# First attention: squares of the head outputs and their products with root and gate on Pool for three of four token tiles

## The chip, the cores and the metric

The kernel runs on one core of a Trainium2 chip. The core has five engines that run side by side and meet at semaphores: TensorE (PE in the profile), VectorE (DVE), ScalarE (ACT), GpSimd (POOL) and SyncE (SP, which issues loads here). The metric is the device time of one execution in microseconds (us), lower is better.

## The reference, cut to what matters

The program is a whole model of three blocks: a differential attention, a latent attention (MLA), and a block with dilated attention, convolution and 32 experts, on 512 tokens of width 1024. The change touches only the end of the first attention:

```
def _diff_attention(h, positions, ...):
    ...
    def block(qb):
        sc = einsum('bqhcd,bkhcd->bhcqk', qb, k) * scale
        p = softmax(sc, axis=-1)
        p = p[:, :, 0] - lam * p[:, :, 1]
        return einsum('bhqk,bkhd->bqhd', p.astype(v.dtype), v)
    o = _from_blocks(lax.map(block, _to_blocks(q)))
    o = _rmsnorm(o, subln_g) * (1.0 - lambda_init)
    o = o.reshape(b, s, DA_WIDTH) * silu(z)
    return o @ w_out
```

For each token and each of 8 heads, the 128 outputs are squared, summed, turned into one over the root of the mean, and multiplied with that root and with the gate silu(z). All is float32.

## The kernel before, in words

The work is staged for one core with weights streamed through a ring of slots. The first attention runs in 32 steps, one for each pair of token tile t (4 tiles of 128 tokens) and head h (8). Each engine has its own program; what follows is the order in which each issues one step i.

PE (`attention`, lines 650 to 680): the scores of step i + 2 (line 795, two banks of 512 columns), four transposes of the combined probabilities of step i (line 601), and the product with V of step i - 1 (line 799). When i is 6 in a tile (OUT_AT), it also transposes the gated outputs of the tile before (`out_tile`, line 722 waits for `og_ready`, then eight transposes at line 601), between the transposes and the product.

DVE (`attention`, lines 1738 to 1749): the row maxima of step i + 1 (`maxima0`, line 1821, 1024 columns from PSUM), then `combine0` of step i: a reciprocal (line 1828), a small product (line 1829, two inputs and a scalar in SBUF), and the difference of the two softmaxes (line 1832, 512 columns, two inputs in SBUF) which PE's transposes of step i wait for. Then `post0` of step i - 2 (line 1838): the head output from PSUM into `o_raw`.

ACT: the exponentials of step i + 1 (line 1155) and copies of the transposes (line 1164; line 1179 for gated outputs).

In `post0`, when h is 7, DVE also squares the 1024 columns of the tile (line 1846, into `bufE`) and sums them by head (line 1847, into `ss`). POOL waits for the sums and makes the root in six small instructions on 8 columns (`rstd`, lines 1409 to 1419). When h is 1 in the next tile, DVE calls `finish_heads`: eight products of 128 columns, o_raw times root times gate into `D_tok` (line 1856), then `og_ready` (line 1859). For the last tile `finish_heads` follows at once.

POOL otherwise does little here: its program around the change is the two stores of zeros (line 1440), then the loop over four tiles with `norm_rstd` (line 1443), then the roots of the later norms. SP's queue waits for `og_ready` only at line 523, for the 12th of its increments in the whole kernel.

In the rows, buffers have the names of the tensors that hold them: `slots` holds `o_raw`, `bufE`, the probabilities and V; `bufD` holds `D_tok` under its own view; `mix` holds the combined probabilities, `pw` and `ss` the small columns of the roots.

Of the kernel before, what the change touches and what calls it, by code (L numbers as in the profile page):

```python
# [10 lines left out]
ALU = mybir.AluOpType  # L11
ACT = mybir.ActivationFunctionType
AX = mybir.AxisListType

P = 128
T = 512
TT = T // P
D = 1024
# [3 lines left out]
HEADS = 8  # L22
# [20 lines left out]
MAIN = sum(ROWS_OF)  # L43
LN_AT = 4
OUT_AT = 6
PAIRS_OUT_AT = 3
GATED = ((0, slice(0, T // 2)), (1, slice(0, T // 2)), (0, slice(T // 2, T)), (1, slice(T // 2, T)), (2, slice(0, T)), (3, slice(0, T)))
OVER = 16
# [90 lines left out]
def fused_kernel(nc, a, out, xs, ys):  # L139

    with ExitStack() as ctx:
# [3 lines left out]
        def sem(name):  # L145
            return ctx.enter_context(nc.semaphore(name))
# [9 lines left out]
        bufE = slots[:, late:late + 2560]  # L156
# [21 lines left out]
        ss = sb("ss", [P, 16])  # L178
# [29 lines left out]
        C_tok, D_tok = tok(bufC), tok(bufD)  # L208
        o_raw = hT.rearrange("p b n -> p (b n)").rearrange("p (t n) -> p t n", t=TT)
# [88 lines left out]
        squares_ready, rstd_ready = sem("squares_ready"), sem("rstd_ready")  # L298
# [6 lines left out]
        max_ready, exp_ready, mix_ready = sem("max_ready"), sem("exp_ready"), sem("mix_ready")  # L305
        og_ready, oT_ready, convT_ready = sem("gated_output_ready"), sem("outputT_token_tile_ready"), sem("convT_ready")
        raw1_ready, n1_ready, nT_ready = sem("latents_ready"), sem("latents_normed"), sem("latentsT_ready")
        qk_ready = sem("qk_ready")
        norm_row_in, norm_row_used = sem("norm_row_loaded"), sem("norm_row_used")
        alibi_in = sem("alibi_loaded")  # L310
        sig_ready, u_used = sem("sigmoid_ready"), sem("sigmoid_used")
# [1087 lines left out]
        def _(pool):  # L1399
            steps = Steps(pool, pool_step)  # L1400
            gp = nc.gpsimd
# [21 lines left out]
            def norm_rstd(width=D, cols=TT, arrivals=TT, lo=0):  # L1423
                nonlocal count
                count += arrivals
                pool.wait_ge(squares_ready, count)
                rstd(cols, width, lo)

            def tile_rstds(*cols):
                for col in cols:  # L1430
                    norm_rstd(D, 1, 1, col)
# [6 lines left out]
            for rows in (xs[:, :], ys[MAIN:, :]):  # L1438
                blocks = rows.rearrange("(p m) d -> p m d", p=ZERO_P)
                gp.dma_start(blocks, norm_row[0:ZERO_P, :].unsqueeze(1).to_broadcast([ZERO_P, blocks.shape[1], D]))\  # L1440
                    .then_inc(zeros_out, 16)
            for t in range(TT):
                norm_rstd(128, 8, 1)
            tile_rstds(0, 1, 2, 3)
            norm_rstd(1, 8, 1)
            tile_rstds(0, 1, 4, 5, 2, 6, 3, 7)
# [40 lines left out]
        def _(dve):  # L1487
# [11 lines left out]
            def wait_rstd():  # L1499
                rstds[0] += 1  # L1500
                dve.wait_ge(rstd_ready, rstds[0])
# [333 lines left out]
            def post0(i):  # L1835
                t, h = i // HEADS, i % HEADS
                bank = dve_banks.take(dve)
                v.tensor_scalar(o_raw[:, t, h * P:(h + 1) * P], bank[:, 0:P], inv_sums[:, 2 * i:2 * i + 1], None,
                                ALU.mult).then_inc(dve_freed, 1)
                if h == 1 and t > 0:  # L1840
                    finish_heads(t - 1)
                if h == HEADS - 1:

                    dve.wait_ge(dve_freed, dve_banks.n)
                    sq = bufE[:, 0:D]
                    chain(v.tensor_tensor(sq, o_raw[:, t, :], o_raw[:, t, :], ALU.mult))
                    v.tensor_reduce(ss[:, 0:8], sq.rearrange("p (h d) -> p h d", h=HEADS), AX.X, ALU.add)\
                        .then_inc(squares_ready, 1)
                    if t == TT - 1:
                        finish_heads(t)  # L1850

            def finish_heads(t):
                wait_rstd()
                for h in range(HEADS):
                    zt = D_tok[:, t, h * P:(h + 1) * P]
                    steps(v.scalar_tensor_tensor(out=zt, in0=o_raw[:, t, h * P:(h + 1) * P], scalar=ss[:, h:h + 1],
                                                 in1=zt, op0=ALU.mult, op1=ALU.mult))
                steps.settle()
                dve.sem_inc(og_ready, 1)
# [338 lines left out]
```

## Time and profile before

| | |
|---|---|
| median of 3 runs | 1653.33 us (1652.55 to 1653.66) |
| the profiled execution's own time | 1656.97 us |
| its span, first to last instruction | 1655.2 us |
| busy in the span | PE 1424.4 us, DVE 644.3, ACT 357.5, POOL 103.5 |
| first attention, first maxima to last head output | 277.0 to 384.8 us |
| mean granted TensorE clock | 0.936 of full speed |

The profile is one execution; its time is 3.6 us over the median, and what it is read for is the length and order of things inside it. Times in rows are us from the start of the span. In a timeline row the columns are start, duration, engine, line, operation, what it writes and reads, and in brackets the engine's idle time just before with the instruction that ended it. In a row of stretches, each engine has its busy time and number of instructions, then PEclk (the granted TensorE clock, 1.00 is full speed, 2.4 GHz), the busy share of the DMA engines and GB/s.

### The profile page before, as it was taken

The numbers are of one execution on the slowest core, as the hardware profiler recorded it, in microseconds if no ns is written. First come the engines' busy times: TensorE is split into PE (matmuls) and PEld (weight loads), VectorE is DVE, ScalarE is ACT, GpSimd is POOL, SyncE is SP. The second block draws the span as 40 slices with busy tenths as digits, with TensorE's granted clock in tenths as the row PEclk, the third lists the DMA queues.
The fourth block names the chain that finished last, engine by engine and source line by source line (L and its number), as shares of the span: only waits on it lengthen the run. The fifth ranks groups of instructions, "written<-read, shape, count | busy, mean of one in ns | idle before, by whom it ended". The sixth has DMA issues, their size and how long they took to land.

```text
span 1655.2 us, 17036 instructions
## 1 busy us (share of the span) xinstructions
PE 1424.4 (86%) x6498; PEld 724.4 (44%) x6498; DVE 644.3 (39%) x1170; ACT 357.5 (22%) x778; POOL 103.5 (6%) x236
## 2 busy tenths in 40 slices
PE   4999999889899999999899989969986876968770
PEld 2544444554455444664654456424432333423330
DVE  4664102994357413322489763242211111111113
ACT  2434002762311143431400163100000000000001
POOL 3000000010100000001100000120000000000004
PEclk9999999999999899999899989979998989979985
DMA  9762224920267431002424123269999999999984
GB/s 341 272 212 81 97 102 158 313 61 1 92 230 236 154 135 69 1 1 102 155 74 152 51 102 153 76 230 395 413 400 409 407 406 401 417 401 412 401 360 156
DMA packets 101339, 356.98 MB, mean 216 GB/s; under 512 B 9448, under 2 KB 15641, under 8 KB 92681
## 3 DMA queue, kind: packets, MB, share of 16 engines
q1 hardware_dynamic: 82512, 305.15, 48.5%
q0 software_dynamic: 9728, 34.47, 6.2%
q10 hardware_dynamic: 9016, 16.25, 2.7%
q8 instruction: 54, 0.88, 0.2%
q14 instruction: 29, 0.23, 0.0%
HBM read 323.60 MB, written 32.24 MB: 215 GB/s over the span
## 4 chain that ended last, share of the span: by engine, by line
PE 64%; DMA 17%; DVE 11%; ACT 2%; issue 2%; SPq 1%; POOL 1%; ACTq 0%; DVEq 0%; POOLq 0%
PE bank L625 15%; DMA slots<-in_w_exp_up 12%; PE score_banks L617 11%; PE score_banks L1006 9%; PE score_banks L625 9%; DVE bufD L1976 5%; PE bank L601 4%; PE bank L1016 4%; DMA slots<-in_w_exp_gate 2%; PE bank L859 2%; PE score_banks L795 2%; PE score_banks L852 2%; DMA slots<-in_ada_w 2%; PE bank L799 2%; SPq L508 1%
## 5 line engine op out<-in xcount | busy, mean ns | idle before, releaser
L625 PE MATMUL bank<-slots 128*128 128x512 f32 x608 | 265.8, 595 | 4.4 <-ACTq L1182 2.5
L617 PE MATMUL score_banks<-slots 128*128 128x512 f32 (+1 forms) x584 | 249.3, 586 | 11.4 <-ACTq L1108 6.2
L1006 PE MATMUL score_banks<-slots,norm_row 128*64 128x512 f32 (+1 forms) x768 | 174.4, 631 | 54.8 <-DMA slots<-in_w_exp_up 47.4
L625 PEld LDWEIGHTS bank<-slots 128*128 128x128 f32 x608 | 114.4, 191 | 146.7 <-issue 143.4
L617 PEld LDWEIGHTS score_banks<-slots 128*128 128x128 f32 x584 | 114.2, 198 | 139.6 <-issue 129.8
L625 PE MATMUL score_banks<-slots 128*128 128x512 f32 (+1 forms) x384 | 157.3, 570 | 0.6 <-PE bank L625 0.3
L2076 DVE TENSOR_TENSOR mix<-probsT,score_banks 128x256 f32<-128x256 f32 (+1 forms) x39 | 14.4, 370 | 326.6 <-ACT probsT L1374 326.6
L1006 PEld LDWEIGHTS score_banks<-slots,norm_row 128*64 128x64 f32 (+1 forms) x768 | 60.3, 148 | 162.9 <-issue 162.8
L1016 PE MATMUL bank<-slots,mix 128*64 128x512 f32 (+1 forms) x864 | 115.2, 477 | 11.5 <-issue 10.4
L1374 ACT ACTIVATE probsT<-score_banks 128x256 f32<-128x256 f32 (+1 forms) x39 | 13.4, 343 | 464.2 <-PE score_banks L1006 464.2
L625 PEld LDWEIGHTS score_banks<-slots 128*128 128x128 f32 x384 | 74.5, 200 | 77.7 <-issue 77.7
L1006 PE MATMUL score_banks<-slots,mix 128*32 128x256 f32 (+1 forms) x960 | 77.7, 451 | 31.1 <-issue 29.4
L1976 DVE SCALAR_TENSOR_TENSOR bufD<-slots,col,bufD 128x512 f32<-128x512 f32 x120 | 80.5, 746 | 0.4
L1016 PEld LDWEIGHTS bank<-slots,mix 128*64 128x64 f32 (+1 forms) x864 | 45.0, 121 | 66.1 <-issue 60.8
L1006 PEld LDWEIGHTS score_banks<-slots,mix 128*32 128x32 f32 (+1 forms) x960 | 39.7, 127 | 73.2 <-issue 60.7
L1637 DVE SCALAR_TENSOR_TENSOR bufD<-slots,silu_c,bufD 128x512 f32<-128x512 f32 x91 | 68.4, 752 | 4.1 <-DMA slots<-in_w_mod 0.6
L1711 DVE TENSOR_TENSOR mix<-bank,gate_row 128x512 f32<-128x512 f32 x24 | 16.6, 692 | 119.9 <-PE bank L625 119.7
L1821 DVE TENSOR_REDUCE negmax<-score_banks 128x2 f32<-128x1024 f32 x32 | 39.0, 1221 | 61.3 <-PE score_banks L795 60.6
L1637 DVE SCALAR_TENSOR_TENSOR slots<-slots,silu_c 128x512 f32<-128x512 f32 x70 | 52.6, 752 | 11.3 <-DMA slots<-in_w_mod 5.8
L1409 POOL TENSOR_SCALAR pw<-ss 128x1 f32<-128x1 f32 (+2 forms) x27 | 8.1, 299 | 768.0 <-ACT slots L1096 439.7
L601 PE MATMUL bank<-k_sb,slots 128*128 128x128 f32 x312 | 48.0, 297 | 8.0 <-ACTq L1107 3.8
L601 PEld LDWEIGHTS bank<-k_sb,slots 128*128 128x128 f32 x312 | 36.7, 150 | 32.1 <-issue 19.5
(295 smaller groups left out, 1480.9 us busy)
## 6 DMA issues: line engine op xcount, KB each, us to landing
slots<-in_w_exp_down SPq DMA_DIRECT2D x32, 2048.0 KB, 36.1
slots<-in_w_exp_gate SPq DMA_DIRECT2D x32, 2048.0 KB, 30.4
slots<-in_w_exp_up SPq DMA_DIRECT2D x32, 2048.0 KB, 32.7
slots<-in_w_in SPq DMA_DIRECT2D x16, 2048.0 KB, 8.6
slots<-in_w_mod SPq DMA_DIRECT2D x24, 1024.0 KB, 5.2
slots<-in_ada_w SPq DMA_DIRECT2D x18, 1024.0 KB, 7.2
expert_rows<-norm_row POOLq DMA_DIRECT2D x1, 12672.0 KB, 50.4
slots<-in_w_out SPq DMA_DIRECT2D x6, 2048.0 KB, 7.9
```

Of the source, the lines that this page charges most:

```text
L601: last = nc.tensor.transpose(bank[:, i * P:(i + 1) * P], piece, ident)
L617: last = mm(bank[:, cols], w[:, k, lo:lo + P], src[:, k, cols], start=(k == 0), stop=(k == kts - 1))
L625: last = mm(bank[:, 0:cols], src[:, k, t * P:(t + 1) * P], rhs(k), start=(k == 0), stop=(k == kts - 1))
L795: return mm(bank[:, :], A8[r, h, t * P:(t + 1) * P], B8[r, h, :], start=True, stop=True)
L799: last = mm(bank[:, 0:P], pT[:, j * P:(j + 1) * P], C_tok[:, j, h * P:(h + 1) * P], start=(j == 0), stop=(j == TT - 1))
L852: mm(bank[:, :], hT[:, 2 * pair + c, t * P:(t + 1) * P], A8[:, 2 * pair + c, :], start=True, stop=False)
L859: last = mm(bank[:, c * P:(c + 1) * P], pT[:, j * P:(j + 1) * P], C_tok[:, j, h * P:(h + 1) * P], start=(j == 0), stop=(j == TT - 1))
L1006: last = mm(out, rows[:, k, :], e_gu[it.p][:, :, k, c * pc.ff:(c + 1) * pc.ff], start=(k == 0), stop=(k == KT - 1))
L1016: last = mm(psum[6 + pc.bank][c * pc.size:(c + 1) * pc.size, 0:pc.cols], hTe[pc.bank][:, lo:lo + pc.size], e_down[it.p][:, f, c * pc.cols: ...
L1637: return v.scalar_tensor_tensor(out=acc, in0=w, scalar=c, in1=acc, op0=ALU.mult, op1=ALU.add)
L1821: v.tensor_reduce(negmax[:, 2 * i:2 * i + 2], pair, AX.X, ALU.max, negate=True).then_inc(max_ready, 1)
L1976: conv_at[j] = steps(v.scalar_tensor_tensor(out=conv[:, j, :], in0=src, scalar=wcol, in1=conv[:, j, :], op0=ALU.mult, op1=ALU.add))
```

## The change

For tiles 0 to 2, the squares and the products with root and gate go from DVE to POOL. DVE signals `heads_ready` after the tile's last head output. POOL then squares the tile in one instruction of 1024 columns into `bufE`. DVE sums the squares two steps later, behind the post of head 1 of the next tile (`SQUARES_AT`), after waits on the squares and, from tile 2 on, on an earlier `og_ready`. POOL makes the root as before, then multiplies `o_raw` with the root (1024 columns, in place, root broadcast along 128 columns), waits for that, and multiplies `D_tok` with it (1024 columns), which raises `og_ready`. Tile 3 stays on DVE.

```
--- before.py
+++ after.py
@@ -43,6 +43,7 @@
 MAIN = sum(ROWS_OF)
 LN_AT = 4
 OUT_AT = 6
+SQUARES_AT = 1
 PAIRS_OUT_AT = 3
 GATED = ((0, slice(0, T // 2)), (1, slice(0, T // 2)), (0, slice(T // 2, T)), (1, slice(T // 2, T)), (2, slice(0, T)), (3, slice(0, T)))
 OVER = 16
@@ -305,7 +306,8 @@
         max_ready, exp_ready, mix_ready = sem("max_ready"), sem("exp_ready"), sem("mix_ready")
         og_ready, oT_ready, convT_ready = sem("gated_output_ready"), sem("outputT_token_tile_ready"), sem("convT_ready")
         raw1_ready, n1_ready, nT_ready = sem("latents_ready"), sem("latents_normed"), sem("latentsT_ready")
-        qk_ready = sem("qk_ready")
+        qk_ready, heads_ready = sem("qk_ready"), sem("heads_of_tile_ready")
+        head_squares = sem("squares_of_heads_ready")
         norm_row_in, norm_row_used = sem("norm_row_loaded"), sem("norm_row_used")
         alibi_in = sem("alibi_loaded")
         sig_ready, u_used = sem("sigmoid_ready"), sem("sigmoid_used")
@@ -1440,7 +1442,16 @@
                 gp.dma_start(blocks, norm_row[0:ZERO_P, :].unsqueeze(1).to_broadcast([ZERO_P, blocks.shape[1], D]))\
                     .then_inc(zeros_out, 16)
             for t in range(TT):
+                if t < TT - 1:
+                    pool.wait_ge(heads_ready, t + 1)
+                    gp.tensor_tensor(bufE[:, 0:D], o_raw[:, t, :], o_raw[:, t, :], ALU.mult).then_inc(head_squares, 1)
                 norm_rstd(128, 8, 1)
+                if t < TT - 1:
+                    heads = o_raw[:, t, :].rearrange("p (h d) -> p h d", h=HEADS)
+                    pool.wait_ge(rstd_ready, 2 + t)
+                    steps(gp.tensor_tensor(heads, heads, ss[:, 0:8].unsqueeze(2).to_broadcast([P, HEADS, P]), ALU.mult))
+                    steps.settle()
+                    gp.tensor_tensor(D_tok[:, t, :], D_tok[:, t, :], o_raw[:, t, :], ALU.mult).then_inc(og_ready, 1)
             tile_rstds(0, 1, 2, 3)
             norm_rstd(1, 8, 1)
             tile_rstds(0, 1, 4, 5, 2, 6, 3, 7)
@@ -1837,19 +1848,28 @@
                 bank = dve_banks.take(dve)
                 v.tensor_scalar(o_raw[:, t, h * P:(h + 1) * P], bank[:, 0:P], inv_sums[:, 2 * i:2 * i + 1], None,
                                 ALU.mult).then_inc(dve_freed, 1)
-                if h == 1 and t > 0:
-                    finish_heads(t - 1)
+                if h == SQUARES_AT and t > 0:
+                    if t > 1:
+                        dve.wait_ge(og_ready, t - 1)
+                    dve.wait_ge(head_squares, t)
+                    sum_squares()
                 if h == HEADS - 1:
-
                     dve.wait_ge(dve_freed, dve_banks.n)
+                    if t < TT - 1:
+                        dve.sem_inc(heads_ready, 1)
+                        return
                     sq = bufE[:, 0:D]
                     chain(v.tensor_tensor(sq, o_raw[:, t, :], o_raw[:, t, :], ALU.mult))
-                    v.tensor_reduce(ss[:, 0:8], sq.rearrange("p (h d) -> p h d", h=HEADS), AX.X, ALU.add)\
-                        .then_inc(squares_ready, 1)
-                    if t == TT - 1:
-                        finish_heads(t)
+                    dve.wait_ge(og_ready, t)
+                    sum_squares()
+                    finish_heads(t)
+
+            def sum_squares():
+                v.tensor_reduce(ss[:, 0:8], bufE[:, 0:D].rearrange("p (h d) -> p h d", h=HEADS), AX.X, ALU.add)\
+                    .then_inc(squares_ready, 1)
 
             def finish_heads(t):
+                rstds[0] += t
                 wait_rstd()
                 for h in range(HEADS):
                     zt = D_tok[:, t, h * P:(h + 1) * P]
```

## Rows read from the trace of the kernel before

**Rows 1.** The page's first line: the span of the profiled execution.

```profile
span 1655.2 us, 17036 instructions
```

**Rows 2.** Stretches between the squares of one tile and the next: length, busy us per engine, PEclk.

```profile
307.70:334.31 26.61, 21.68 (x138) 14.15 (x137) 24.46 (x51) 17.63 (x43) 2.67 (x6) 1.00 0.90 287
334.31:361.41 27.10, 23.19 (x138) 15.52 (x137) 24.55 (x50) 17.52 (x43) 2.65 (x6) 0.94 0.25 77
361.41:384.40 22.99, 18.14 (x117) 13.81 (x116) 18.84 (x40) 12.65 (x30) 2.65 (x6) 0.93 0.00 1
```

**Rows 3.** Timeline, undisturbed attention step on PE and DVE (start us, us, engine, line, op).

```profile
302.47 1.22 DVE L1821 TENSOR_REDUCE negmax<-score_banks 128x2 f32<-128x1024 f32 x1
...
303.79 1.13 PE L795 MATMUL score_banks<-slots 64*128 64x512 f32 x4
303.81 0.22 DVE L1829 SCALAR_TENSOR_TENSOR inv_sums<-inv_sums,lam,sums 128x1 f32<-128x1 f32 x1
304.06 0.75 DVE L1832 SCALAR_TENSOR_TENSOR mix<-slots,inv_sums 128x512 f32<-128x512 f32 x1
...
304.73 0.35 DVE L1838 TENSOR_SCALAR slots<-bank,inv_sums 128x128 f32<-128x128 f32 x1
...
305.06 1.23 DVE L1821 TENSOR_REDUCE negmax<-score_banks 128x2 f32<-128x1024 f32 x1
...
306.35 1.13 PE L795 MATMUL score_banks<-slots 64*128 64x512 f32 x4
```

**Rows 4.** PE's waits between 277 and 388 us: total, times, longest.

```profile
PE bank L601 <- DVE mix L1832: 12.9, 7, 2.4
```

**Rows 5.** Timeline around tile 0's squares and products.

```profile
307.70 1.23 DVE L1846 TENSOR_TENSOR slots<-slots 128x1024 f32<-128x1024 f32 x1
...
308.96 1.22 DVE L1847 TENSOR_REDUCE ss<-slots 128x8 f32<-128x1024 f32 x1
310.10 1.21 DVE L1821 TENSOR_REDUCE negmax<-score_banks 128x2 f32<-128x1024 f32 x1
...
312.48 0.66 PE L601 MATMUL bank<-k_sb,mix 128*128 128x128 f32 x4 [2.41 <-DVE mix L1832]
...
312.60 1.22 DVE L1821 TENSOR_REDUCE negmax<-score_banks 128x2 f32<-128x1024 f32 x1
...
315.11 2.18 DVE L1856 SCALAR_TENSOR_TENSOR bufD<-slots,ss,bufD 128x128 f32<-128x128 f32 x8
...
317.50 1.22 DVE L1821 TENSOR_REDUCE negmax<-score_banks 128x2 f32<-128x1024 f32 x1 [0.21 <-DVE bufD L1856]
```

**Rows 6.** One-microsecond stretch after tile 1's squares (PEclk is the third last number).

```profile
339.00:340.00 1.00, 0.92 (x5) 0.92 (x6) 1.00 (x3) 0.40 (x2) 0.69 (x4) 0.50 0.49 152
```

**Rows 7.** Timeline of POOL, three of six instructions for tile 0's root.

```profile
310.28 0.20 POOL L1409 TENSOR_SCALAR pw<-ss 128x8 f32<-128x8 f32 x1 [31.14 <-DVE ss L1847]
310.56 1.67 POOL L1411 TENSOR_TENSOR pw<-pw,half_neg 128x8 f32<-128x8 f32 x1
...
313.17 0.20 POOL L1419 TENSOR_TENSOR ss<-pw 128x8 f32<-128x8 f32 x1
```

**Rows 8.** POOL's product by shape, between 420 and 1100 us (busy us, mean ns).

```profile
L1415 POOL TENSOR_TENSOR pw<-pw 128x1 f32<-128x1 f32 x16 | 3.1, 191 | 1.3
```

**Rows 9.** The same line by shape, between 277 and 394 us.

```profile
L1415 POOL TENSOR_TENSOR pw<-pw 128x8 f32<-128x8 f32 x4 | 0.8, 203 | 0.3
```

**Rows 10.** Timeline of POOL near 782 us: two small instructions that ran long.

```profile
781.90 1.28 POOL L1409 TENSOR_SCALAR pw<-ss 128x1 f32<-128x1 f32 x1
...
784.71 0.74 POOL L1419 TENSOR_TENSOR ss<-pw 128x1 f32<-128x1 f32 x1
```

**Rows 11.** Timeline of DVE over the same moments.

```profile
781.85 1.28 DVE L1626 SCALAR_TENSOR_TENSOR x<-x,ss,norm_row 128x1024 f32<-128x1024 f32 x1 [1.81 <-POOL ss L1419]
...
784.71 0.69 DVE L1714 TENSOR_TENSOR x<-x,mix 128x512 f32<-128x512 f32 x1
```

**Rows 12.** Timeline, DVE's first reduction after the output transposes of tile 0.

```profile
329.13 1.23 DVE L1821 TENSOR_REDUCE negmax<-score_banks 128x2 f32<-128x1024 f32 x1 [0.81 <-PE score_banks L795]
```

## The prediction

> **What bounds the kernel now.** I read the page first: the span is 1655.2 us [rows 1], and the profiled execution took 1656.97 us against a median of 1653.33. I make the sums as differences from the profiled execution and carry them over to the median; the 3.64 us between the two are not explained by anything here and drop out. Then I cut the attention into its three periods from one tile's squares to the next one's. They last 26.61, 27.10 and 22.99 us, the last one without most of the scores of a next tile [rows 2]. DVE is busy in more than nine tenths of the first two, PE in some 22 of 27 us.
>
> Next the timeline of one quiet step. PE begins the scores every 2.56 us. DVE begins its maxima every 2.59 us, and goes from maxima to the small product in 1.34 us, to the difference in another 0.25, to the head output in 0.67, to the next maxima in 0.33 [rows 3]. Behind a disturbance DVE repeats in 2.50 us (310.10 to 312.60) [rows 5]. So the two engines are tied: DVE can catch up 0.06 us a step and no more, and whatever is put into DVE's step, PE waits for. The waits say so: PE stood 12.9 us in 7 waits for the difference, the longest 2.4 [rows 4].
>
> The timeline shows where. The squares and their sum hold DVE from 307.70 to 310.10, and PE's next transposes sit idle 2.41 us. The eight products hold it from 315.11 to 317.50 [rows 5]. That is 2.40 + 2.39 = 4.79 us of DVE a tile, three times (tile 3's come when no step is behind them). There is a second price. After tile 1's squares the granted clock is 0.50 [rows 6], which is 1.2 GHz instead of 2.4, after PE had stood for 2.4 us. The mean clock of the periods says that tile 2 has the same and tile 0 not (1.00, 0.94, 0.93), and the second period is 27.10 - 26.61 = 0.49 us longer than the first [rows 2]. I take 0.49 us for each of two tiles.
>
> **What the change removes and adds on DVE.** Removed a tile: the squares, 1.26 us from their start to that of the sum, and the products, 2.39. The sum stays and moves two steps back, at its 1.14 us from start to start [rows 5]. Net 1.26 + 2.39 = 3.65 us a tile, 10.95 in all. With the sum alone PE stands about 1.1 us rather than 2.4, so the clock may hold too: 0.98 more. If POOL cost nothing, the kernel would be 11.9 us faster. Tile 3 changes nothing but two waits on things long done. The semaphore increment for POOL takes the place of a wait that is there already; I put it at nothing, and at the 0.04 us between two instructions if it isn't. No DMA is added or moved. SP's wait is for the 12th `og_ready`, which still comes from the second attention. On POOL's queue the three products stand ahead of the next roots, whose squares come from ACT some 40 us later: nothing.
>
> **What POOL's instructions cost.** No row has POOL multiply 1024 columns. Its product takes 191 ns on one column [rows 8] and 203 ns on eight [rows 9], so 12 ns for 7 columns, 1.7 ns a column, and 1.95 us for 1024 as an estimate. From below, I see no reason for POOL to beat DVE's 1.22 us for the same shape [rows 5]. From above, 4 ns more in so small a difference would make it 2.5, and I go to 2.6. I take 1.95, since it comes from the same operation on the same engine. The Trainium skill (GPSIMD Engine Reference, section Elementwise, side-by-side cycle accounting) gives 4497 ns for a two-input product of 2048 columns; an estimate by it is 2.25 us, and by that the forecast below would be 2.7 us later. No run here shows it.
>
> Is that time hidden? By waits alone, yes. The squares have from 307.8 until DVE's sum about 5 us later. The roots take from 310.28 to 313.37, 3.1 us [rows 7], and begin 0.1 us after the sum. The sum would begin at 312.8 and end at 314.0; the root is there at 317.2, and two products by 321.3. PE wants them after the transposes of step 6. DVE's difference for that step is two steps and 1.34 + 0.25 + 0.75 us behind the sum's 1.14: 312.8 + 1.14 + 5.0 + 2.34 = 321.3, and the transposes take 0.66 more. So `og_ready` comes 0.6 us early, and at 2.3 us a product just in time. Behind those output transposes DVE stands idle for 0.81 us [rows 12], which would cover a delay; POOL's products are over by then, so it covers none of theirs.
>
> **The port.** What isn't hidden is in the trace far from here. At 781.90 a POOL instruction on one column took 1.28 us instead of 0.19, and at 784.71 another took 0.74 [rows 10]. In those moments DVE ran instructions with two SBUF inputs, 781.85 to 783.13 and 784.71 to 785.40 [rows 11]: POOL's ended when DVE's did, within 0.05 us. So these two exclude each other for the whole of the first one. The rows show only POOL waiting, because POOL's own instructions there are too short to hold DVE. The new ones are long. I take it that the exclusion holds the other way: DVE's small product and difference wait until a POOL product that has begun is over. Maxima, sum and head output have one tensor input, and I let them run on: POOL's instruction at 310.28 lay inside DVE's maxima and took its usual 0.20 us [rows 5, 7].
>
> The Trainium skill says the same and more (SBUF — State Buffer, section Who interferes with whom): the pair of ports is locked for the whole instruction, whoever starts first, and a DVE instruction with two SBUF inputs meets only POOL instructions that read SBUF. The first half agrees with the rows above; the other direction no row here shows.
>
> Worked out for one tile:
> - Squares: POOL starts at 307.8, ends 309.75. DVE's small product is due 1.34 us behind the maxima at 307.7, at 309.04. Delay 0.71.
> - Product with the root: it starts 0.1 + 3.1 + 0.1 = 3.3 us behind the sum's end, that is 4.5 behind its start. DVE has by then done the 1.14 of the sum and 2.50 of one step, so it is 0.86 into a step, 0.48 before the small product. Delay 1.95 - 0.48 = 1.47.
> - Product with the gate: it is issued 0.09 us behind the other, while the small product (0.22 us) runs, and gets the port as that ends, just ahead of the difference, which is due 0.25 us after the small product began. Delay 1.9.
>
> Together 4.1 us against the 3.65 taken away: +0.45 us a tile, +1.35 in three. PE stands 3.4 us in one piece in each tile, longer than the 2.4 after which the clock fell in two of three tiles, so I take the fall in all three: +0.5. Each handing over of the port may cost up to 0.05 us, and is left out. Sum **+1.9 us**, 1655.2.
>
> **The rivals.**
> 1. *No lock against DVE.* DVE's instructions run on beside POOL's long reads. For it: no row shows DVE late behind POOL, and beside the root's power instruction of 1.67 us [rows 7] DVE kept its 2.50 us step (though on 8 columns the reads may be over at once). Against: [rows 10, 11]. Price: -11.9, less up to 0.5 where POOL waits for DVE and `og_ready` is late: 1641.4 to 1642.
> 2. *The difference takes the port ahead of the second product.* 0.05 us decide it. Then the gate product runs from 1.0 to 2.95 us behind the first one's end and meets the next small product at 2.5, for 0.45 us. Delays 0.71 + 1.47 + 0.45 = 2.6, net -1.0 a tile, -3.0 in all: 1650.3. With products of 2.3 us it is 1.06 + 1.82 + 0.80 = 3.7 and 1653.5.
> 3. *POOL is slower than its slope says.* Every further 0.1 us counts three times a tile, 0.9 us in all. The line from the same to slower is crossed at 2.1 us a product. At 2.6: delays 1.36 + 2.12 + 2.55 = 6.0, net +2.4 a tile, +7.1, and the clock: 1661. Broadcasting the root or writing in place are the likeliest reasons.
> 4. *POOL late for PE.* Without the lock this begins at 2.3 us a product and costs twice the excess; with it PE is later anyway. It only trims rival 1.
>
> **How the numbers follow.** A measurement of this kernel can tell about 0.2%, 3.3 us, from no change. Forecast (lock, gate product first, 1.7 to 2.2 us a product, -0.4 to +4.1): 0.40. Rival 1: 0.20. Rival 2: 0.20, half of it beyond -3.3. Rival 3: 0.20, all slower. Of the forecast 0.10 lies beyond +3.3. So faster 0.20 + 0.10, and 0.02 from smaller delays than worked out: 0.32; slower 0.20 + 0.10 = 0.30; same 0.38. The range holds rival 1 at its lower end and rival 3 up to 2.5 us a product: 1641.3 to 1660. The forecast's own range is 1652.9 to 1657.4.
>
> **What the profile after would show.** On POOL, nine products of 1024 columns, about 1.95 us each; longer ones have waited for DVE. DVE's small product and difference starting more than 1.4 us behind their maxima in the steps of those nine. PE's transposes idle for about 0.7 and 3.4 us a tile. The three periods at 27.6, 27.6 and 23.4 us instead of those of [rows 2]; by rival 1 at 23.0, 23.0 and 18.9. I am wrong if DVE keeps its 2.5 us steps while a POOL product runs, or if those products aren't between 1.7 and 2.2 us.

## The result, and the profile after

| | before | after |
|---|---|---|
| median | 1653.33 us (11 runs beside those of after: 1650.62 to 1656.5) | 1657.95 us (11 runs: 1655.28 to 1661.52) |
| ratio | | 1.0029, 95% interval 1.0019 to 1.0040 |
| the profiled execution's own time, its span | 1656.97, 1655.2 us | 1657.03, 1655.2 us |
| first maxima to last head output | 107.5 us | 111.6 us |
| of it, behind the last head output of tile 0 | 77.1 us | 81.8 us |
| time at half clock, 300 to 392 us | 6.8 us | 17.1 us |

The changed kernel's median is 4.6 us higher, 0.29%. That is little: the kernel before, run against itself (e9 below), came out 0.22% apart. The two spans happen to be equal, so the span says nothing; the attention does. From the start of the first maxima to that of the last head output it is 4.1 us longer, 275.9 to 387.5; counted from the last head output of tile 0, behind which the change does its first work, it is 4.7 us longer. The last line of the table adds up what is missing to 1.00 in the granted clock of the one-microsecond stretches from 300 to 392 us, doubled, since each missing piece fell to 0.50.

The page's first lines, the span and the busy time of each engine (share, instructions):

```profile
span 1655.2 us, 17021 instructions
...
PE 1424.4 (86%) x6498; PEld 724.0 (44%) x6498; DVE 644.9 (39%) x1143; ACT 357.5 (22%) x778; POOL 122.8 (7%) x245
```

POOL gained 19 us, and DVE, which lost 10.2 us of squares and products, is as busy as before (644.9 against 644.3). The DVE instructions grouped by line and shape, 277 to 396 us, show where it went (count, then busy us and mean ns of one):

```profile
L1843 DVE SCALAR_TENSOR_TENSOR mix<-slots,inv_sums 128x512 f32<-128x512 f32 x32 | 30.5, 954 | 1.1
L1840 DVE SCALAR_TENSOR_TENSOR inv_sums<-inv_sums,lam,sums 128x1 f32<-128x1 f32 x32 | 11.5, 358 | 1.1
```

The difference took 752 ns each before and the small product 220. Times 32 that is 6.5 and 4.4 us in which DVE's instructions stood begun and blocked. The same view of POOL, 277 to 400 us:

```profile
L1454 POOL TENSOR_TENSOR bufD<-bufD,slots 128x1024 f32<-128x1024 f32 x3 | 7.0, 2339 | 0.2
...
L1452 POOL TENSOR_TENSOR slots<-slots,ss 128x1024 f32<-128x1024 f32 x3 | 5.7, 1896 | 0.2
L1447 POOL TENSOR_TENSOR slots<-slots 128x1024 f32<-128x1024 f32 x3 | 5.7, 1892 | 57.3 <-DVEq L1859 57.3
```

Tile 0 in the timeline, with the steps of three of those nine products:

```profile
306.22 1.89 POOL L1447 TENSOR_TENSOR slots<-slots 128x1024 f32<-128x1024 f32 x1 [28.13 <-DVEq L1859]
...
306.29 1.23 DVE L1832 TENSOR_REDUCE negmax<-score_banks 128x2 f32<-128x1024 f32 x1 [0.21 <-DVE slots L1849]
...
307.62 0.50 DVE L1840 SCALAR_TENSOR_TENSOR inv_sums<-inv_sums,lam,sums 128x1 f32<-128x1 f32 x1
...
308.97 0.66 PE L603 MATMUL bank<-k_sb,mix 128*128 128x128 f32 x4 [0.49 <-DVE mix L1843]
...
315.11 0.66 PE L603 MATMUL bank<-k_sb,mix 128*128 128x128 f32 x4 [0.99 <-DVE mix L1843]
...
316.08 1.90 POOL L1452 TENSOR_TENSOR slots<-slots,ss 128x1024 f32<-128x1024 f32 x1
...
316.55 1.44 DVE L1840 SCALAR_TENSOR_TENSOR inv_sums<-inv_sums,lam,sums 128x1 f32<-128x1 f32 x1
...
318.03 2.91 DVE L1843 SCALAR_TENSOR_TENSOR mix<-slots,inv_sums 128x512 f32<-128x512 f32 x1
318.05 2.34 POOL L1454 TENSOR_TENSOR bufD<-bufD,slots 128x1024 f32<-128x1024 f32 x1
320.86 0.34 DVE L1849 TENSOR_SCALAR slots<-bank,inv_sums 128x128 f32<-128x128 f32 x1
...
320.99 1.12 PE L603 MATMUL bank<-k_sb,mix 128*128 128x128 f32 x4 [3.28 <-DVE mix L1843]
...
321.90 1.92 PE L801 MATMUL bank<-slots,probsT 128*128 128x128 f32 x8
...
323.75 2.08 PE L797 MATMUL score_banks<-slots 64*128 64x512 f32 x4
...
325.97 1.22 DVE L1832 TENSOR_REDUCE negmax<-score_banks 128x2 f32<-128x1024 f32 x1 [1.76 <-PE score_banks L797]
```

Read it in pairs. The squares end at 308.11, and so does the small product, which took 0.50 instead of 0.22: 0.28 late. The product with the root runs from 316.08 to 317.98, and the small product at 316.55 ends with it: 1.22 late. The product with the gate starts at 318.05, between the small product's end and the difference; DVE's next instruction starts at 320.86, 2.83 behind the difference's start, where 0.67 is usual [rows 3]: 2.16 late. A DVE instruction that waits for the port is shown as long, not as idle, which is why the busy time of 644.9 us hides it. None of the three blocked instructions is late by all of the wait: the small products end 0.01 us behind POOL's product and not their usual 0.22, the difference 0.55 behind and not 0.75. It is as if about 0.2 us of each had run while it waited. Then PE: 0.49, 0.99 and 3.28 us idle. PE's waits from 277 to 392 us, beside [rows 4], and the periods beside [rows 2]:

```profile
PE bank L603 <- DVE mix L1843: 14.2, 9, 3.3
```

```profile
306.22:335.48 29.26, 24.25 (x138) 15.87 (x137) 24.76 (x41) 17.52 (x42) 8.80 (x10) 0.88 0.89 277
335.48:363.74 28.26, 23.29 (x138) 15.37 (x137) 24.73 (x41) 17.52 (x42) 8.79 (x9) 0.94 0.18 59
363.74:387.48 23.74, 19.01 (x116) 15.06 (x115) 18.91 (x31) 12.69 (x29) 8.79 (x9) 0.86 0.00 1
```

And the clock from the gate product on (PEclk is the third number from the end):

```profile
318.00:319.00 1.00, 0.00 (x0) 0.00 (x0) 0.97 (x1) 0.00 (x0) 0.95 (x1) 1.00 0.98 319
...
320.00:321.00 1.00, 0.01 (x1) 0.01 (x1) 1.00 (x2) 0.00 (x0) 0.39 (x1) 0.50 0.98 348
...
325.00:326.00 1.00, 1.00 (x3) 0.25 (x2) 0.03 (x1) 0.00 (x0) 0.00 (x0) 0.50 0.79 238
...
327.00:328.00 1.00, 0.75 (x7) 0.55 (x6) 0.93 (x4) 0.98 (x2) 0.00 (x0) 1.00 0.75 176
```

PE stood from 317.7 to 320.99, and the clock went to 0.50, 1.2 GHz, for some 6.8 us, in a tile that had none of it before. The four transposes then took 1.12 us instead of 0.66, the product with V 1.92 instead of 1.06, the scores 2.08 instead of 1.13. Now DVE waits for PE: 1.76 us before its maxima at 325.97, and 0.41 before the head output ahead of them. In tile 0 before, DVE has no wait in that step. The first period is 2.65 us longer than before, and only 0.22 of it is DVE's own.

### The profile page after: what moved, and what is told of

The parts are those of the page before. It is cut to its first block, busy times and chain, and to the rows that moved or that the text cites. A ratio compares the mean times of both kernels' runs of the same rounds, so it can differ in the third digit from the quotient of the medians.

```text
span 1655.2 us, 17021 instructions
## 1 busy us (share of the span) xinstructions
PE 1424.4 (86%) x6498; PEld 724.0 (44%) x6498; DVE 644.9 (39%) x1143; ACT 357.5 (22%) x778; POOL 122.8 (7%) x245
## 4 chain that ended last, share of the span: by engine, by line
PE 62%; DMA 17%; DVE 14%; issue 3%; ACT 3%; SPq 1%; POOL 1%; ACTq 0%; DVEq 0%; POOLq 0%
PE bank L627 15%; DMA slots<-in_w_exp_up 12%; PE score_banks L619 10%; PE score_banks L1008 10%; PE score_banks L627 9%; DVE bufD L1996 5%; PE bank L1018 4%; PE bank L603 3%; DMA slots<-in_w_exp_gate 2%; DVE negmax L1832 2%; PE bank L861 2%; PE score_banks L854 2%; DMA slots<-in_ada_w 2%; SPq L510 1%; DVE mix L1843 1%
## 5 line engine op out<-in xcount | busy, mean ns | idle before, releaser
L619 PEld LDWEIGHTS score_banks<-slots 128*128 128x128 f32 x584 | 113.2, 196 | 140.2 <-issue 130.1
```

Source lines behind the costliest of these rows:

```text
L619: last = mm(bank[:, cols], w[:, k, lo:lo + P], src[:, k, cols], start=(k == 0), stop=(k == kts - 1))
```

## The experiments

The ratios are against runs of the kernel before on the same chip and in the same series; its median there was 1653.61 us beside e1 to e4, 1654.22 beside e5 to e8, 1655.92 beside e9 and e10, and 1654.43 beside e11. So medians of different series are compared by their ratios. "DVE balance" is worked out for one tile from each trace, as a mean over tiles 0 to 2: what DVE is spared (squares 1.26, products 2.39, less 1.13 where it keeps one product) against what its small product and difference took longer than 0.22 and 0.75 us, and 0.21 for the signal behind a tile's last head output, which e2 and e4 don't have. A plus means more time on DVE. "Attention" is first maxima to last head output, "behind tile 0" the part of it from the last head output of tile 0, "half clock" as above.

| run | median us | ratio, 95% interval | attention us | behind tile 0, us | DVE balance a tile, us | half clock us |
|---|---|---|---|---|---|---|
| before | 1653.33 | | 107.5 | 77.1 | 0 | 6.8 |
| after | 1657.95 | 1.0029 (1.0019 to 1.0040) | 111.6 | 81.8 | +0.20 | 17.1 |
| e1 squares only | 1658.01 | 1.0027 (1.0015 to 1.0040) | 106.3 | 77.5 | -0.77 | 10.2 |
| e2 products only | 1657.05 | 1.0023 (1.0009 to 1.0037) | 110.9 | 80.8 | +0.96 | 10.3 |
| e3 memsets | 1642.38 | 0.9927 (0.9910 to 0.9945) | 96.0 | 65.7 | -3.44 | 0 |
| e4 idle products | 1663.57 | 1.0050 (1.0032 to 1.0068) | 116.7 | 87.6 | +2.09 | 13.6 |
| e5 placed | 1648.34 | 0.9963 (0.9945 to 0.9981) | 99.1 | 68.7 | -2.31 | 0 |
| e6 unplaced | 1659.43 | 1.0025 (1.0011 to 1.0039) | 108.9 | 78.5 | +0.02 | 10.3 |
| e7 a step earlier | 1653.84 | 0.9996 (0.9980 to 1.0012) | 107.5 | 77.1 | -0.77 | 10.2 |
| e8 is e1 again | 1656.92 | 1.0011 (0.9995 to 1.0027) | 106.3 | 77.5 | -0.77 | 10.2 |
| e9 is before again | 1651.86 | 0.9978 (0.9968 to 0.9988) | 107.4 | 77.1 | 0 | 6.8 |
| e10 is after again | 1658.56 | 1.0018 (1.0007 to 1.0029) | 111.1 | 80.8 | +0.20 | 13.6 |
| e11 is e5 again | 1644.89 | 0.9955 (0.9935 to 0.9976) | 97.8 | 68.7 | -2.31 | 0 |

Read the column "behind tile 0", not "attention". Up to the last head output of tile 0 all versions run the same program, and still that part took 28.8 to 29.0 us in four traces (e1, e4, e8, e11), with 3.4 us at half clock in it, and 29.8 to 30.4 in the other nine, with 6.8. Nothing in the edits explains which.

**e3, the same signals and waits, but POOL only writes.** Each product becomes two memsets (the squares are shown; root and gate are changed alike):

```
-  gp.tensor_tensor(bufE[:, 0:D], o_raw[:, t, :], o_raw[:, t, :], ALU.mult).then_inc(head_squares, 1)
+  steps(gp.memset(bufE[:, 0:D], 1.0))
+  steps.settle()
+  gp.memset(bufE[:, 0:D], 1.0).then_inc(head_squares, 1)
...
```

> The changed kernel with each of POOL's products replaced by two memsets of 1024 columns one after the other (about 0.95 us each), so the squares, the root and the gate are left out of tiles 0 to 2. All signals and waits stay, and POOL is busy as long, but reads nothing from SBUF. Port theory: DVE isn't held, PE stands only for the sum, the clock stays up: about 11 us faster than before, 1641 to 1644. Waits theory: as the changed kernel, 1658.

11.2 us faster than before, as the port theory had it. In its timeline POOL is as busy in the steps concerned, and the small product at 308.15 and the difference at 308.40 run at their usual length beside it:

```profile
306.72 0.95 POOL L1447 MEMSET slots<- 128x1024 f32 x1 [28.63 <-DVEq L1863]
...
307.73 0.95 POOL L1449 MEMSET slots<- 128x1024 f32 x1
...
308.15 0.22 DVE L1844 SCALAR_TENSOR_TENSOR inv_sums<-inv_sums,lam,sums 128x1 f32<-128x1 f32 x1
308.40 0.75 DVE L1847 SCALAR_TENSOR_TENSOR mix<-slots,inv_sums 128x512 f32<-128x512 f32 x1
```

DVE's only new wait is 0.21 us at the next maxima. So beyond those 0.21 neither the waits nor a busy POOL cost anything. What a memset lacks is POOL's reading, and it is a different operation too; that a read is what holds is the plainest account of e3 and e4 together.

**e4, the kernel before with two idle POOL products a tile.** Nothing is taken off DVE and nobody waits for POOL; `scratch` is a part of `bufE` that nobody reads:

```
+  if t < TT - 1:
+      pool.wait_ge(heads_ready, t + 1)
+      steps(gp.tensor_tensor(scratch, o_raw[:, t, :], o_raw[:, t, :], ALU.mult))
+      steps.settle()
+      steps(gp.tensor_tensor(scratch, o_raw[:, t, :], C_tok[:, t, :], ALU.mult))
...
+  if h == 3 and t > 0:
+      dve.sem_inc(heads_ready, 1)
```

> The kernel before, with nothing taken from DVE, and two more products of 1024 columns on POOL in each of three tiles, into a buffer nobody reads, started by one signal behind head 3. The first has the same tensor as both inputs, the second two different ones. Port theory: the first holds DVE's small product 0.3 to 0.6 us, the second holds the difference about 2.2 us, and PE's idle piece of 2.5 to 3 us is followed by half clock: +7.5 to +8.5 us by the delays, with the clock +9 to +13: 1662 to 1666. Waits theory: one signal a tile, +0 to +0.6 us. The second product's length says whether 2.34 us (against 1.89) comes from its two different inputs; if it takes 1.9 here, the gate product's length in the change came from DVE.

10 us slower by the medians, 8.3 by the ratio, and 10.5 us behind tile 0, for work that is thrown away. That is inside the 1662 to 1666 expected. The timeline shows both directions of the exclusion:

```profile
318.99 0.75 DVE L1839 SCALAR_TENSOR_TENSOR mix<-slots,inv_sums 128x512 f32<-128x512 f32 x1
319.10 2.39 POOL L1447 TENSOR_TENSOR slots<-slots 128x1024 f32<-128x1024 f32 x1 [8.34 <-DVEq L1850]
...
321.37 0.22 DVE L1836 SCALAR_TENSOR_TENSOR inv_sums<-inv_sums,lam,sums 128x1 f32<-128x1 f32 x1
321.57 2.35 POOL L1449 TENSOR_TENSOR slots<-slots 128x1024 f32<-128x1024 f32 x1
321.62 2.84 DVE L1839 SCALAR_TENSOR_TENSOR mix<-slots,inv_sums 128x512 f32<-128x512 f32 x1
```

POOL's first product starts 0.11 us behind DVE's difference and takes 2.39 us, some 0.5 more than its like elsewhere (1.89): it waited for DVE. Its second begins at 321.57, as DVE's small product ends, and the difference at 321.62 takes 2.84 instead of 0.75. One part of the expectation missed: the first product was to hold the small product 0.3 to 0.6 us, and the small product at 321.37 kept its 0.22, as POOL was nearly done by then (321.49). Another part was answered: the second product took 2.35 us here too (2.34 in the other tiles), so its length comes from its two different inputs and not from DVE. e3 and e4 together settle the port theory for these instructions, which the prediction had from one direction only.

**e1 and e2, one part alone.** e1 leaves the squares on POOL and has DVE do its eight products two steps behind the sum (POOL's two products are gone); e2 has the squares on DVE as before and both products on POOL. Of e1's edit against the changed kernel:

```
...
   if h == SQUARES_AT and t > 0:
-      if t > 1:
-          dve.wait_ge(og_ready, t - 1)
       dve.wait_ge(head_squares, t)
       sum_squares()
+  if h == SQUARES_AT + 2 and t > 0:
+      finish_heads(t - 1)
...
```

> POOL squares tiles 0 to 2, DVE sums them behind head 1 and makes the eight products behind head 3. Port theory (a DVE instruction with two SBUF inputs waits until a POOL product that has begun is over, and nothing else costs): of the change's three delays a tile (0.3, 1.2 and 2.2 us) only the first is left, against 1.26 us taken from DVE; with 0.2 us for the new signal that is about -0.8 us a tile, and PE's longest idle piece falls, which may save the half clock too: -2.3 to -3.5 us, 1650 to 1651. Waits theory (the new signals and waits between POOL and DVE cost the time, whatever POOL runs): no faster than before, 1653 or more.

> Squares and sum stay on DVE, POOL makes the two products of 1024 columns with root and gate. Port theory: the product with the root begins some 0.5 us ahead of DVE's small product and holds it about 1.4 us, the product with the gate holds the difference about 2.2 us, against 2.39 us taken away: +1.2 us a tile and a longer time at half clock, +4 to +6 in all, 1657 to 1659, as slow as the whole change or slower. Waits theory: there is one signal fewer than in the whole change, so between before and after.

e2 came out about as expected, at the lower end (+0.96 us a tile against +1.2, and +3.4 us by the medians against +4 to +6), and with +3.6 us behind tile 0 it has most of the change's loss. e1 missed. By its time alone the waits theory would have been right (1653 or more); e3 is what excludes it. The squares cost DVE only the 0.28 us foreseen, and yet nothing is gained. Its timeline shows where the gain went:

```profile
317.32 2.18 DVE L1868 SCALAR_TENSOR_TENSOR bufD<-slots,ss,bufD 128x128 f32<-128x128 f32 x8
...
322.11 0.94 PE L603 MATMUL bank<-k_sb,mix 128*128 128x128 f32 x4 [2.27 <-DVE mix L1837]
...
322.84 2.01 PE L603 MATMUL bank<-k_sb,bufD 128*128 128x128 f32 x8
...
326.28 0.35 DVE L1843 TENSOR_SCALAR slots<-bank,inv_sums 128x128 f32<-128x128 f32 x1 [1.72 <-PE bank L801]
```

The products behind head 3 make PE wait 2.27 us just ahead of the output transposes. The clock falls, the eight output transposes take 2.01 us where e5 has 0.60 + 0.66, and DVE waits 1.72 us for the product behind them. So 2.3 us of spared DVE time became nothing: behind tile 0 e1 takes 0.4 us more than before. Its whole attention is 1.1 us shorter only because the part ahead of that, where the program is the same, took 1.5 us less. Nor does the attention explain that the median is 1658.01.

**e7, e8, e9, how much of this is real.** e7 is e1 with `SQUARES_AT = 0`, so that the products come a step earlier; e8 is e1, e9 is the kernel before and e10 the kernel after, word for word.

> As the kernel with the squares alone on POOL, but the sum comes behind head 0 and DVE's eight products behind head 2, one step earlier. Theory (that kernel lost its gain because the 2.3 us for which PE stands for the eight products end right before the output transposes of step 6, and the half clock that follows falls on the stretch where PE alone sets the pace): one step earlier the fall lies mostly ahead of them, so 1 us a tile is won: 1651 to 1655. Rival (POOL's squares or the signals cost more than the trace shows): the same 1658.

> The kernel with the squares alone on POOL once more, for a second trace. Its profiled execution was at 1655.6 us, 2.4 under its median. Theory: the executions differ by how often and how long the granted clock falls to half in the attention; a trace nearer to the median has longer periods of attention than 26.91, 26.95 and 23.33 us. Rival: the attention is as long as before and the difference lies elsewhere.

> The kernel before, word for word, against itself: what two equal kernels differ by, and a second trace. Two traces of the kernel with the squares alone on POOL both show 106.3 us from the first maxima to the last head output, and before showed 107.4, while that kernel was measured 0.1 to 0.3% slower than before. If the clock falls by chance in this stretch, the second trace of before is 104 to 106 us there (one or no fall to half) and explains it. If it is 107.4 again, the attention is fixed from execution to execution and the difference is in the measurement or behind the attention. The ratio should be 1.000 within 0.0015.

> The changed kernel once more, for a second trace and ratio: 111.6 us from the first maxima to the last head output if the stretch is fixed, and 1.002 to 1.004 times before.

e7 did not do what it was made for: behind tile 0 it is 0.4 us shorter than e1, not 1 us a tile. The half clock now slows the scores of the next step, and DVE waits 1.41 us for them. Still its time fell into the range expected, 0.3% better than e1 by the ratios, and 0.15% better than e1's repetition e8. e9 says how far such a figure goes: a kernel against itself gave 0.9978 where 1.000 within 0.0015 was expected, 3.6 us by the ratio and 4.1 by the medians, with an interval that leaves out 1. The stated intervals are too narrow for differences of 0.2%. The traces are steadier. Behind tile 0 before repeats within 0.1 us, e1 and e5 too (77.1, 77.5 and 68.7 us in both traces of each); the change has 81.8 and 80.8, with 17.1 and 13.6 us at half clock. So e8's theory, that e1's executions differ by the attention, fell. The stretches behind the attention, where the text is the same, scatter (from the squares of the second block's latents to its first maxima 140.2 to 143.6 us over the runs). Whether e1 is slower than before stays open. The change's own loss is seen twice, in ratio (1.0029, 1.0018) and behind tile 0 (+4.7, +3.7). The ratios alone would not show it, with equal kernels 0.22% apart; the traces do.

**e5 and e6, where POOL's products lie.** Both square on POOL, have POOL multiply the gate in before the root is known instead of behind it, and leave DVE one product with the root (1.13 us instead of 2.39). e6 issues both POOL instructions at once; e5 cuts the squares in halves, starts the first behind the last head output, and holds the second half and the gate product back until a difference of the attention is done:

```
+  pool.wait_ge(heads_ready, t + 1)
+  steps(gp.tensor_tensor(sq[:, 0:half], o[:, 0:half], o[:, 0:half], ALU.mult))
+  pool.wait_ge(mix_ready, 8 * t + 11)
+  gp.tensor_tensor(sq[:, half:D], o[:, half:D], o[:, half:D], ALU.mult).then_inc(head_squares, 1)
+  pool.wait_ge(mix_ready, 8 * t + 12)
+  gp.tensor_tensor(D_tok[:, t, :], D_tok[:, t, :], o, ALU.mult).then_inc(gated_raw, 1)
...
+  v.tensor_tensor(zt, zt, ss[:, 0:8].unsqueeze(2).to_broadcast([P, HEADS, P]), ALU.mult).then_inc(og_ready, 1)
```

> Port theory turned into a version. POOL squares the tile in two halves of 512 columns (about 1 us each), the first right behind the last head output, the second behind the next step's difference (a wait on mix_ready), and multiplies gate by raw heads (1024 columns, 2.34 us) behind the difference of the step in which DVE sums the squares, so each lies beside DVE's maxima, sum and head output and holds no instruction with two SBUF inputs. DVE multiplies by the root in one instruction of 1024 columns behind head 3. DVE then has 1.14 + 1.3 us a tile instead of 4.79, with 0.2 for the signal: -2.1 us a tile, -6 us, and less time at half clock because PE's idle pieces are 1.1 and 1.3 us: 1645 to 1648. Rival (any reading POOL product costs DVE its own length, wherever it lies): no faster than before.

> The same work split as in the version with placed products, but POOL squares all 1024 columns and multiplies by the gate at once behind the last head output, with no wait on mix_ready. Port theory: the squares hold the small product 0.3 us, the gate product meets the next small product for about 0.7 us, so about 1 us a tile more than the placed version, with half clock up to 4 us more in all: 1648 to 1652. Rival (placing doesn't matter): equal to the placed version within 1 us.

e5 beats both kernels: 1648.34 us, 5.9 us under the kernel before in the same series (1654.22), ratio 0.9963 where the change has 1.0029. It was expected at 1645 to 1648, about 6 us under before. In its timeline every POOL product lies between a difference and the next small product, or beside the sum and the maxima, and DVE keeps 0.22 and 0.75:

```profile
307.27 1.04 POOL L1449 TENSOR_TENSOR slots<-slots 128x512 f32<-128x512 f32 x1 [28.69 <-DVEq L1862]
...
308.67 0.22 DVE L1840 SCALAR_TENSOR_TENSOR inv_sums<-inv_sums,lam,sums 128x1 f32<-128x1 f32 x1
308.92 0.75 DVE L1843 SCALAR_TENSOR_TENSOR mix<-slots,inv_sums 128x512 f32<-128x512 f32 x1
...
309.76 1.03 POOL L1451 TENSOR_TENSOR slots<-slots 128x512 f32<-128x512 f32 x1 [1.46 <-DVE mix L1843]
...
312.26 2.36 POOL L1453 TENSOR_TENSOR bufD<-bufD,slots 128x1024 f32<-128x1024 f32 x1 [1.47 <-DVE mix L1843]
...
312.36 1.21 DVE L1871 TENSOR_REDUCE ss<-slots 128x8 f32<-128x1024 f32 x1
...
314.80 0.22 DVE L1840 SCALAR_TENSOR_TENSOR inv_sums<-inv_sums,lam,sums 128x1 f32<-128x1 f32 x1
```

e6 missed by 7 to 11 us. I had the gate product meet the next small product for 0.7 us. It did something else, which the prediction's second rival had also left to chance:

```profile
307.11 1.89 POOL L1447 TENSOR_TENSOR slots<-slots 128x1024 f32<-128x1024 f32 x1 [28.76 <-DVEq L1857]
...
308.51 0.50 DVE L1835 SCALAR_TENSOR_TENSOR inv_sums<-inv_sums,lam,sums 128x1 f32<-128x1 f32 x1
308.98 2.33 POOL L1448 TENSOR_TENSOR bufD<-bufD,slots 128x1024 f32<-128x1024 f32 x1
...
309.05 2.80 DVE L1838 SCALAR_TENSOR_TENSOR mix<-slots,inv_sums 128x512 f32<-128x512 f32 x1
```

The gate product was already queued on POOL when the squares ended at 309.00. DVE's small product ended with them, at 309.01, so the gate product didn't hold it; but POOL had the port before the difference, which started 0.05 us later. In the change, in e2, e4, e6 and e10, each time in all three tiles, a waiting POOL product slipped in between DVE's two instructions.

**e11, the placed version once more.** Edit: none against e5.

> The placed version e5 once more, word for word, since two equal kernels (e9) lay 0.2% apart, and e5's gain was 0.4%. If the gain is real: an attention of 99 us again, 8 us shorter than before, and a ratio of 0.994 to 0.998. If it was scatter of the rest of the program: a ratio over 0.998, with the same short attention.

1644.89 us against 1654.43, ratio 0.9955. The gain is there twice, in time and in attention, and is about twice the scatter that e9 showed. Its attention is 1.3 us shorter than e5's, but behind tile 0 the two agree at 68.7 us, 8.4 less than before: the difference lies ahead of the first squares, in the attention's first 25 us (mean clock 0.93 against 0.86), not in what was edited.

## Why the prediction was right, and where it was off

The prediction said 1655.2 us, 1.9 over the median of before. Measured were 1657.95, 4.6 over it, and 4.7 us more behind tile 0 (3.7 in e10). That lies inside the full range, 1641.3 to 1660, which was wide enough for most rivals too, and just outside the forecast's own, 1652.9 to 1657.4. The mechanism is the one forecast, and e3 and e4 show it: the exclusion holds against DVE, and the DVE instructions that suffer are the two with two SBUF inputs. The Trainium skill's rule (SBUF — State Buffer, section Who interferes with whom) speaks of a GpSimd instruction that reads SBUF, not of one that only writes; the traces agree on both halves, 2.91 us for a difference behind a product, and 0.75 beside a memset. That the sum came so near is partly luck: the work on DVE was forecast too dear and the clock too cheap.

Step by step:

- **Removed work, 3.65 us a tile.** Right. e3, where only that and the signal are left, is 11.4 us shorter behind tile 0; 3 x 3.44 = 10.3 and the clock's 1.0 make 11.3.
- **POOL's product, 1.95 us.** Right for the squares and the root (1.89 and 1.90), too low for the gate (2.34), which is outside the 1.7 to 2.2 that the prediction named as a sign of being wrong. The slope from one to eight columns led near the mark where both inputs are one tensor, or one is a broadcast root; with 12 ns to draw it from, that was partly luck. With two different tensors the product took 2.34 us in the change and in e2, 2.33 to 2.35 in e6, and 2.34 to 2.35 in e4's second product. The estimate of 2.25 us by the Trainium skill (GPSIMD Engine Reference, section Elementwise) lies near that one, and the trace disagrees with it for the other two. Rival 3 had broadcasting or writing in place as the likeliest reasons for a slow POOL; the product with the root does both and took 1.90.
- **Delays of 0.71, 1.47 and 1.9, 4.1 together.** They were 0.28, 1.22 and 2.16, 3.66 in tile 0. POOL's products began where they were forecast, the root's 0.47 us ahead of the small product (0.48 forecast) and the squares 0.2 us sooner. What the forecast left out is the 0.2 us by which a blocked DVE instruction ends sooner behind POOL's product than its own length. The gate's product was longer.
- **The signal, 0.04 us at most.** It cost 0.21 us a tile: the next maxima stood idle that long behind the head output. An increment alone doesn't: in e4 the one behind head 3 leaves the usual 0.04 us to the next maxima (319.66 + 0.34 to 320.04). The change's stands behind a wait for DVE's own last write.
- **Balance.** 3.66 + 0.21 - 3.65 = +0.22 in tile 0, +0.20 as a mean of the three, against +0.45 forecast: +0.6 in all against +1.35. That part is better than forecast.
- **The clock, +0.5.** This is the step that failed. It is what the balance leaves, 4.7 - 0.6 = 4.1 us (3.1 in e10). The stall was foreseen (3.4 in one piece, measured 3.28), and so was a fall of the clock in all three tiles. What I took for its price was the difference of two periods of before, 0.49 us, where the fall followed 2.4 us of idling, lasted some 3.4 us, and DVE stood still for 0.4 us at most. After 3.3 us of idling it lasted 6.8 us in tiles 0 and 2 but 3.4 in tile 1 (in e10 6.8, 3.4 and 3.4), and PE at half speed became the slower of the two engines: DVE waited 2.2 us for it in tile 0 and 1.6 in tile 1. A stall's length doesn't settle it: in tile 0 of before 2.41 and 2.27 us of idling left the clock at 1.00, and in e1 2.27 us were followed by 3.4 us at half clock. In the table the rest of each change behind tile 0, once three balances are taken off, goes roughly with the time at half clock: -1.1 to -1.5 us without any (e3, e5, e11), +0.8 to +2.7 at 10 us (e1, e2, e6, e7, e8), +3.1 and +4.3 at 13.6 (e10, e4), +4.1 at 17 (after).
- **Periods of 27.6, 27.6, 23.4.** They were 29.26, 28.26 and 23.74: the excess is the clock, largest in the tile that had kept it before.
- **What to look for in the profile.** The small product was to start more than 1.4 us behind its maxima. It started at the usual 1.33 (306.29 to 307.62) and was long instead, as POOL's held instructions were in [rows 10].
- **Rival 1, no lock:** excluded, by the rows above and by e3 landing within 0.4 us of where it put the whole change (1641.4 to 1642; e3 measured 1642.38). **Rival 2, the difference first:** didn't happen in any of the fifteen chances of the change, e2, e4, e6 and e10. **Rival 4, POOL late for PE:** didn't happen; `og_ready` came at 320.4, PE's output transposes at 326.60.

The traces leave 0.8 us over behind the attention, between the last of tile 3's products and the squares of the next block's latents (107.9 us before, 107.7 in e9, 108.7 after). e1, e2, e3, e5 and e6 have 108.6 to 108.8 there too, e4, e10 and e11 108.9 to 109.1, e7 108.2 and e8 108.4; its cause wasn't looked for.

## What to carry to other kernels

Work moved from DVE to GpSimd isn't hidden because GpSimd is idle: for as long as it reads SBUF, DVE's next instruction with two SBUF inputs waits for its end, and the trace shows that as a long DVE instruction, not as a wait. Count where each GpSimd instruction falls in DVE's step; cut to fit and released by a semaphore of DVE's own step, the same work gave 0.4% (e5, e11) where issued at once it cost 0.25% (e6). And price a stall of PE with the clock behind it: in the change DVE's extra work came to 0.6 us, and what went with the half clock to 4.1.

## What was unexpected

- A POOL product of 1024 float32 columns took 1.89 us with one tensor as both inputs, 1.90 with a root broadcast along 128 columns, and 2.34 with two different tensors; 512 columns of one tensor took 1.04.
- A POOL product already waiting got the port between two DVE instructions that usually start 0.25 us apart, fifteen times in fifteen in tiles 0 to 2 of the change, e2, e4, e6 and e10.
- About the same time at half clock, 10.2 to 10.3 us, went with +0.8 us in e2, +1.3 in e6, +2.3 in e7 and +2.7 in e1, balances taken off. What PE had to do then differs: in e1 the output transposes took 2.01 us, in e7 the product with V 1.91. That this is the reason is argued, not shown.
- The attention up to tile 0's last head output, the same program in all versions, took 28.8 to 29.0 us or 29.8 to 30.4, and made e1 look 1.1 us faster than before.
- A kernel against itself measured 0.9978 with an interval of 0.9968 to 0.9988.
